# Attention steps of the engines shifted, and the scaling of the probabilities on GpSimd

## The chip, the core and the metric

One core of a Trainium2 chip runs the whole program. The metric is the device time of one execution in microseconds (us). Five engines run streams of their own and meet only in semaphores: TensorE (PE) multiplies and transposes, VectorE (DVE), ScalarE (ACT) and GpSimd (POOL) work on tiles of 128 partitions, SyncE (SP) issues most of the transfers. Inputs and results are f32 in HBM.

## The reference, cut to what matters

Two layers and one larger block over 512 positions of width 1024. Every attention that matters here is a softmax over at most 512 keys of each of 512 queries:

```python
s = einsum('bcqhd,bckhd->bhcqk', qc, kb) * (d ** -0.5)   # each layer: 6 heads "A" with a bias table,
s = where(valid, s + bias, NEG)                           # 5 heads "C" and 5 heads "B" (256 chosen keys)
p = jax.nn.softmax(s, axis=-1)
o = einsum('bhcqk,bckhd->bcqhd', p, vb)
# block 2: 16 heads "Fox", causal, with a decay
logits = einsum('bhqd,bhkd->bhqk', qi, k) * scale + (fi[..., :, None] - cum_f[..., None, :])
y_fox = softmax(where(k_pos <= q_pos, logits, -inf)) @ v
```

Around them stand feed-forward parts, projections of the input with `w_in`, a stick-breaking attention, a linear recurrence and gates; the change does not touch those.

## The kernel before, in words

**Numbers.** Each f32 product is made of three products of rounded parts (high times high, high times low, low times high; L214 to L216). So each operand is split: ScalarE writes the high part, another engine subtracts and writes the low part.

**Steps.** An attention is a list of steps, one for each head and each block of 128 queries. The four steps of a head have 128, 256, 384 and 512 keys (TT is 4). A layer runs 24 steps for heads A (`a_steps`) and, after the projection of C, 40 steps for heads C and B (`cb_steps`). Block 2 runs 64 steps for Fox (`fox_steps`). A step m goes through seven stages:

1. TensorE: the scores, three matmuls (L1012 to L1014), a fourth for Fox (L1016).
2. VectorE: mask, copy to SBUF, negated row maximum (L1094).
3. ScalarE: exponential with the row sum (L1057).
4. VectorE: reciprocal of the sum (L1101), drain (L1102), scaling of the probabilities in place (L1103).
5. TensorE: transposes of the blocks of 128 keys into a PSUM bank (L1039).
6. ScalarE: high part of the transposed block (L1074).
7. VectorE: low part (L1109).

After the four steps of a head TensorE makes the head's values from the transposed parts, twelve matmuls (L1028 to L1031).

**Order.** Each engine has its own function with a loop over n: `attend_pe_parts`, `attend_act_parts`, `attend_dve_parts`. In pass n of the kernel before, TensorE does the scores of step n, the values of a head when n is 3 mod 4, and the transposes of step n-3 (LAG is 3). ScalarE does the exponential of n, splits of the next pair of heads where n is 5 or 6 mod 8 (`split_act`), and the high part of n-3. VectorE does the row maximum of n, the scaling of n-1 and the low part of n-3. The transposes have two banks to turn in (`n_turned`), the probabilities four buffers (the row maximum of n waits for the transposes of n-4), and the transposed parts of a head one buffer for each part: the first high part of the next head waits for `hv_done`, the values of the head before. GpSimd makes the low parts of the split pairs (`split_pool`, L987), in the layers also the transfers of the bias table (`bias_dma`).

**What is woven in.** In heads A, VectorE also runs a round of the choice of B's keys in each of the first steps (`select_rounds`, maximum and replacement of eight, with drains) and the bias of each head (`bias_dve`). In Fox the attention is woven with 24 projections, "tiles" below, of 24 matmuls each: `woven` hands out a pass of the projection (`project_pe_parts` and its fellows), then a pass of the attention, on every engine in the same pattern; the projection's pass comes first. A projection's pass for tile j holds also what comes after for tiles j-1 and j-2: for a q or k tile a sum of squares on TensorE (L648), a root on ScalarE (L709) with a change of its function table before and after, reciprocal and spread on VectorE (L743, L746), transposes on TensorE (L630), and the scaling on VectorE (L733); for a v tile transposes (L660) and a copy (L756). VectorE's pass begins with the low part of a later weight tile (L206), which waits for ScalarE's high part (L199). Tiles come in the order q, k, v.

Of the kernel before, what the change touches and what calls it, by code (L numbers as in the profile page):

```python
# [16 lines left out]
F32 = mybir.dt.float32  # L17
# [69 lines left out]
def build(nc, A, out):  # L87
# [418 lines left out]
    pl_done = sem("probs_low_ready")  # L506
    hv_done = sem("head_values_used")
# [446 lines left out]
    class Places:  # L954

        def __init__(self, scores, turned, n_turned, probs, parts=None):
            self.scores, self.turned, self.n_turned, self.probs, self.parts = scores, turned, n_turned, probs, parts

# [10 lines left out]
    def layer_places(parts):  # L969
        return Places(lambda n, w: B[n % 2][:, 0:w], lambda m, a, b: B[2 + m % 2][:, a:b], 2,  # L970
                      lambda m, w: (SG[:, 0, 0:w], SG[:, 1, 0:w], TMP[:, 0:w], T[:, 0, 0:w])[m % 4], parts)
# [29 lines left out]

    def attend_pe_parts(pe, steps, n0, l0, h0, s0, y0, at, hook=None, banks=2):
        for n in range(len(steps) + LAG + 1):
# [14 lines left out]
            if n >= LAG + TT and (n - LAG) % TT == 0:  # L1018
                h = (n - LAG) // TT - 1
# [24 lines left out]
    def pair_taken(steps, n):  # L1044

        at = n - LAG - 8
        return at // 8 if at >= 0 and at % 8 == 0 else None

    def attend_act_parts(act, steps, n0, h0, s0, y_of, jobs, waits, at):
        act.drain()  # L1050
        pairs = len(jobs) // 3
        for n in range(len(steps) + LAG + 1):
            if n < len(steps):
# [4 lines left out]
                               accum_out=SUM[:, n % 4:n % 4 + 1]).then_inc(exp_done, 1)  # L1058
                pair = n // 8
# [8 lines left out]
            if LAG <= n < len(steps) + LAG:  # L1068
                m = n - LAG
                w = steps[m]["width"]  # L1070
                act.wait_ge(tr_done, n0 + (m + 3))
                if m % TT == 0:
                    act.wait_ge(hv_done, h0 + (m // TT + 1))
                act.activation(at.block(0, steps[m]), at.turned(m, 0, w).rearrange("p (k c) -> p k c", c=P), ACT.Copy  # L1074
                               ).then_inc(pt_done, 1)
            pair = pair_taken(steps, n)
            if pair is not None:
                act.wait_ge(hv_done, h0 + (2 * pair + 3))
                for bank, dst_hi, dst_lo in y_of(steps[8 * pair]["group"]):
                    act.activation(dst_hi, B[bank][:, :], ACT.Copy).then_inc(y_hi, 1)  # L1080
            yield

    def attend_dve_parts(dve, steps, n0, y0, y_of, at, hook=None):
        dve.drain()
        for n in range(len(steps) + LAG + 1):
# [19 lines left out]
            if LAG <= n < len(steps) + LAG:  # L1105
                m = n - LAG
                w = steps[m]["width"]
                dve.wait_ge(pt_done, n0 + (m + 3))
                dve.tensor_tensor(at.block(1, steps[m]), at.turned(m, 0, w).rearrange("p (k c) -> p k c", c=P),  # L1109
                                  at.block(0, steps[m]).bitcast(F32), ALU.subtract).then_inc(pl_done, 1)  # L1110
            pair = pair_taken(steps, n)
            if pair is not None:
# [256 lines left out]
    def layer_pool(pool, l):  # L1369
# [20 lines left out]
        for j in range(5, 9):  # L1390
            split_pool(pool, a_jobs, j, l * JOBS)
# [985 lines left out]
```

## Time and profile before

| what | value |
|---|---|
| median of 3 runs | 4385.77 us (4383.34 to 4387.92) |
| the profiled execution | 4383.03 us, its span 4381.4 us |
| TensorE busy | 4066.4 us, 93% of the span |
| VectorE busy | 1714.9 us, 39% |
| ScalarE busy | 1505.5 us, 34% |
| GpSimd busy | 369.0 us, 8% |
| mean granted TensorE clock | 0.926 |
| steps of heads A | 607 to 714 us and 1887 to 1996 us |
| steps of heads C and B | 751 to about 869 us and 2030 to 2151 us |
| steps of Fox | 2925 to 3247 us |

The span is cut into stages that follow each other. A share of busy time over the whole span says little of a stage, so each stage is read for itself: busy time and granted clock of its stretch first (the granted clock is 1.00 for 2.4 GHz and 0.50 for 1.2 GHz), then what its engines wait for, then the timeline of a few steps.

### The profile page before, as it was taken

How to read it: one execution, taken by the hardware profiler on the slowest of the kernel's cores; microseconds unless marked ns; L12 is line 12 of the kernel's file. 1: busy time of each engine (PE TensorE's matmuls, PEld its weight loads, DVE VectorE, ACT ScalarE, POOL GpSimd, SP SyncE). 2: the span in 40 equal slices, each digit the busy share in tenths (PEclk: the TensorE clock that was granted, in tenths of full speed). 3: DMA queues.
4: the chain of work that ended last, by engine and by line, in shares of the span. 5: the costliest groups of instructions: out<-in, count | busy, mean ns of one | idle time of the engine just before them, and what ended most of it. 6: DMA issues, size and time to landing. Idle time of an engine off the chain costs nothing.

```text
span 4381.4 us, 51384 instructions
## 1 busy us (share of the span) xinstructions
PE 4066.4 (93%) x17788; PEld 3216.0 (73%) x17788; DVE 1714.9 (39%) x2847; ACT 1505.5 (34%) x2448; POOL 369.0 (8%) x374
## 2 busy tenths in 40 slices
PE   8999978799999999967899989899999999789999
PEld 6887755588878887745688868787777668567888
DVE  3323565433323323664433234334432223534442
ACT  3222323432223223324332234435534553533331
POOL 1100011101001100011011000000100000100110
PEclk9999976799999999968799979999899999899999
DMA  3333310023323323200023324131112113222332
GB/s 102 96 97 97 82 42 20 1 82 96 96 82 91 96 96 93 76 19 20 29 82 96 96 86 112 39 83 44 39 54 72 39 44 91 58 73 76 96 98 98
DMA packets 495308, 316.51 MB, mean 72 GB/s; under 512 B 10832, under 2 KB 476368, under 8 KB 494640
## 3 DMA queue, kind: packets, MB, share of 16 engines
q1 hardware_dynamic: 490992, 302.86, 23.8%
q0 software_dynamic: 3008, 9.57, 0.7%
q8 instruction: 86, 1.41, 0.1%
q10 hardware_dynamic: 1152, 2.10, 0.1%
q14 instruction: 70, 0.57, 0.0%
HBM read 309.77 MB, written 4.33 MB: 72 GB/s over the span
## 4 chain that ended last, share of the span: by engine, by line
PE 68%; issue 21%; DVE 3%; ACT 3%; POOL 2%; PEld 1%; DVEq 1%; POOLq 0%; PEldq 0%; ACTq 0%
PE bank L214 19%; PE bank L216 19%; PE bank L215 19%; PE bank L256 1%; PE bank L1728 1%; PE bank L1734 1%; PE bank L1748 1%; PE bank L1737 1%; POOL h_lo L299 1%; PE bank L1028 1%; PE bank L1039 0%; PE bank L1030 0%; PE bank L1031 0%; PE bank L1149 0%; PE bank L648 0%
## 5 line engine op out<-in xcount | busy, mean ns | idle before, releaser
L214 PE MATMUL bank<-h_hi,w_hi 128*128 128x512 f32 (+3 forms) x3240 | 1297.9, 401 | 58.6 <-DVE w_lo L206 29.8
L215 PE MATMUL bank<-h_hi,w_lo 128*128 128x512 f32 (+3 forms) x3240 | 1279.0, 395 | 0.0
L216 PE MATMUL bank<-h_lo,w_hi 128*128 128x512 f32 (+3 forms) x3240 | 1277.7, 394 | 0.0
L206 DVE TENSOR_TENSOR w_lo<-w_raw,w_hi 128x1024 fp32r<-128x1024 f32 x571 | 737.7, 1292 | 1189.4 <-ACT w_hi L199 1183.4
L199 ACT ACTIVATE w_hi<-w_raw 128x1024 fp32r<-128x1024 f32 x571 | 598.4, 1049 | 596.4 <-DMA w_raw<-in_ffn_w_down 320.0
L214 PEld LDWEIGHTS bank<-h_hi,w_hi 128*128 128x128 f32 (+3 forms) x3240 | 612.1, 189 | 228.0 <-ACT lru_x L1831 31.0
L216 PEld LDWEIGHTS bank<-h_lo,w_hi 128*128 128x128 f32 (+3 forms) x3240 | 611.2, 189 | 140.5 <-issue 3.8
L215 PEld LDWEIGHTS bank<-h_hi,w_lo 128*128 128x128 f32 (+3 forms) x3240 | 612.5, 189 | 134.0 <-issue 4.6
L214 PE MATMUL bank<-g_hi,w_hi 128*128 (+1 forms) x880 | 342.3, 389 | 0.0
L215 PE MATMUL bank<-g_hi,w_lo 128*128 (+1 forms) x880 | 342.3, 389 | 0.0
L216 PE MATMUL bank<-g_lo,w_hi 128*128 (+1 forms) x880 | 342.3, 389 | 0.0
L383 POOL TENSOR_TENSOR g_lo<-gu_ring,g_hi 128x512 f32 x110 | 142.5, 1296 | 1048.2 <-ACT g_hi L357 838.5
L357 ACT ACTIVATE g_hi<-gu_ring 128x512 f32 x88 | 55.7, 632 | 424.0 <-DVE gu_ring L369 424.0
L215 PEld LDWEIGHTS bank<-g_hi,w_lo 128*128 128x128 f32 x880 | 165.2, 188 | 34.4
L214 PEld LDWEIGHTS bank<-g_hi,w_hi 128*128 128x128 f32 x880 | 165.2, 188 | 34.3
L216 PEld LDWEIGHTS bank<-g_lo,w_hi 128*128 128x128 f32 x880 | 165.2, 188 | 34.2
L256 PE MATMUL bank<-ones,s_ring 128*128 128x1 f32 x688 | 124.2, 316 | 38.5 <-ACT s_ring L241 33.2
L256 PEld LDWEIGHTS bank<-ones,s_ring 128*128 128x128 f32 x688 | 123.5, 283 | 43.4 <-ACT s_ring L241 34.6
L369 DVE TENSOR_TENSOR gu_ring<-s_ring,bank 128x512 f32<-128x512 f32 x88 | 60.5, 687 | 241.2 <-PE bank L216 241.2
L354 ACT ACTIVATE s_ring<-bank 128x512 f32<-128x512 f32 x88 | 52.7, 599 | 246.9 <-PE bank L216 246.9
L214 PE MATMUL bank<-branch_hi,w_hi 128*128 128x512 f32 x256 | 101.0, 394 | 13.4 <-POOL branch_lo L1930 13.4
L701 ACT ACTIVATE t_ring<-bank 128x512 f32<-128x512 f32 (+4 forms) x66 | 37.5, 569 | 199.1 <-PE bank L216 163.8
(382 smaller groups left out, 4404.1 us busy)
## 6 DMA issues: line engine op xcount, KB each, us to landing
w_raw<-in_w_in SPq DMA_DIRECT2D x161, 512.0 KB, 3.8
w_raw<-in_ffn_w_gate SPq DMA_DIRECT2D x88, 512.0 KB, 3.8
w_raw<-in_ffn_w_up SPq DMA_DIRECT2D x88, 512.0 KB, 3.8
w_raw<-in_ffn_w_down SPq DMA_DIRECT2D x88, 512.0 KB, 3.5
w_raw<-in_w_up SPq DMA_DIRECT2D x44, 512.0 KB, 3.7
w_raw<-in_w_branch SPq DMA_DIRECT2D x32, 512.0 KB, 3.8
w_raw<-in_w_out SPq DMA_DIRECT2D x24, 512.0 KB, 3.8
w_raw<-in_w_down SPq DMA_DIRECT2D x22, 512.0 KB, 3.5
```

The source lines that it names most:

```text
L199: act.activation(WH[:, slot(c), 0:w], RAW[:, slot(c), 0:w], ACT.Copy).then_inc(w_hi, 1)
L206: dve.tensor_tensor(WL[:, slot(c), 0:w], RAW[:, slot(c), 0:w], WH[:, slot(c), 0:w].bitcast(F32), ALU.subtract).then_inc(w_lo, 1)
L214: pe.matmul(bank, wh, xh, start=start, stop=False)
L215: pe.matmul(bank, wl, xh, start=False, stop=False)
L216: return pe.matmul(bank, wh, xl, start=False, stop=stop)
L256: last = pe.matmul(stat_bank[:, t:t + 1], SG[:, k % 2, t * P:(t + 1) * P], ONE[:, 0:1], start=(k == 0 and t == 0), stop=(k == n - 1), skip ...
L299: pool.tensor_tensor(dst[1](k), scaled_tile(k, n, width), dst[0](k).bitcast(F32), ALU.subtract).then_inc(nm_lo_odd, 1)
L354: act.activation(SG[:, t, :], B[2 * t][:, :], ACT.Silu).then_inc(silu_done, 1)
L357: act.activation(GH[:, i * 2 + t, :], GU[:, t, :], ACT.Copy).then_inc(gh_done, 1)
L369: dve.tensor_tensor(GU[:, t, :], SG[:, t, :], B[2 * t + 1][:, :], ALU.mult).then_inc(gu_done, 1)
L383: pool.tensor_tensor(GL[:, i * 2 + t, :], GU[:, t, :], GH[:, i * 2 + t, :].bitcast(F32), ALU.subtract).then_inc(gl_done, 1)
L1028: pe.matmul(out_, VH[:, kt, cols], at.keys(0, kt), start=(h % 2 == 0 and kt == 0), stop=False, skip_group_check=True)
```

## The change

A fifth function, `attend_pool`, runs on GpSimd, and the scaling of step n-1 moves to its pass n. It waits for the reciprocal (`rc_done`), and the drain ahead of the scaling goes. GpSimd's splits and the transfers of the bias table move into its passes. On the other engines the later stages move back. With n the pass:

| | before | after, layers | after, Fox |
|---|---|---|---|
| ScalarE, high part | n-3, after the splits | n-4, ahead of the splits; the first two steps of a head together in pass 1 mod 4 (`late`) | n-4, ahead of the splits |
| VectorE, low part | n-3, last in the pass | n-5, first in the pass; the first two steps together in pass 2 mod 4 | n-5, first in the pass |
| TensorE, values of a head | pass 3 mod 4 | pass 1 mod 4, two passes later | the same |
| TensorE, transposes of n-3 wait for the low part of | n-5 | n-6 (three banks) | n-5 (two banks) |

The tail has two passes more, and in Fox the 26 passes of the projection are spread over 70 instead of 68 passes.

```diff
     def layer_places(parts):
-        return Places(lambda n, w: B[n % 2][:, 0:w], lambda m, a, b: B[2 + m % 2][:, a:b], 2,
+        return Places(lambda n, w: B[n % 2][:, 0:w], lambda m, a, b: B[(2, 3, 6)[m % 3]][:, a:b], 3,
...
+    def turned_at(m, n, late):
+        if late and m % TT < 2:
+            return [] if m % TT == 0 else [k for k in (m - 1, m) if 0 <= k < n]
+        return [m] if 0 <= m < n else []
     def attend_pe_parts(pe, steps, n0, l0, h0, s0, y0, at, hook=None, banks=2):
-        for n in range(len(steps) + LAG + 1):
+        for n in range(len(steps) + TT + 2):
...
-            if n >= LAG + TT and (n - LAG) % TT == 0:
-                h = (n - LAG) // TT - 1
+            if n > 2 * TT and n % TT == 1:
+                h = n // TT - 2
...
-                pe.wait_ge(pl_done, l0 + (m + 1))
+                pe.wait_ge(pl_done, l0 + (m + 3 - at.n_turned))
...
     def attend_act_parts(act, steps, n0, h0, s0, y_of, jobs, waits, at):
...
+            for m in turned_at(n - TT, len(steps), at.late):
+                w = steps[m]["width"]
+                act.wait_ge(tr_done, n0 + (m + 3))
+                if m % TT == 0:
+                    act.wait_ge(hv_done, h0 + (m // TT + 1))
+                act.activation(at.block(0, steps[m]), at.turned(m, 0, w).rearrange("p (k c) -> p k c", c=P), ACT.Copy
+                               ).then_inc(pt_done, 1)
...
+    def attend_dve_parts(dve, steps, n0, y0, y_of, at, hook=None):
+        dve.drain()
+        for n in range(len(steps) + TT + 3):
+            for m in turned_at(n - TT - 1, len(steps), at.late):
...
                 dve.wait_ge(exp_done, n0 + (m + 1))
-                dve.reciprocal(RSUM[:, m % 4:m % 4 + 1], SUM[:, m % 4:m % 4 + 1])
-                dve.drain()
-                dve.tensor_scalar(at.probs(m, w), at.probs(m, w), RSUM[:, m % 4:m % 4 + 1], None,
-                                  ALU.mult).then_inc(nrm_done, 1)
+                dve.reciprocal(RSUM[:, m % 4:m % 4 + 1], SUM[:, m % 4:m % 4 + 1]).then_inc(rc_done, 1)
...
+    def attend_pool(pool, steps, n0, l0, s0, jobs, at, hook=None):
+        pairs = len(jobs) // 3
+        for n in range(len(steps) + 1):
+            if hook:
+                hook(pool, n)
+            if n >= 1:
+                m = n - 1
+                w = steps[m]["width"]
+                pool.wait_ge(rc_done, l0 + (m + 1))
+                pass_wait(pool)
+                pool.tensor_scalar(at.probs(m, w), at.probs(m, w), RSUM[:, m % 4:m % 4 + 1], None,
+                                   ALU.mult).then_inc(nrm_done, 1)
+            if n < len(steps):
+                pair = n // 8
+                if n % 8 == 5 and pair > 0:
+                    split_pool(pool, jobs, 3 * pair + 2, s0)
+                if n % 8 == 5 and pair + 1 < pairs:
+                    split_pool(pool, jobs, 3 * (pair + 1), s0)
+                if n % 8 == 6 and pair + 1 < pairs:
+                    split_pool(pool, jobs, 3 * (pair + 1) + 1, s0)
...
-    MEM_STEPS_AND_TAIL, FOX_STEPS_AND_TAIL = 16 + LAG + 3, 64 + LAG + 1
+    MEM_STEPS_AND_TAIL, FOX_STEPS_AND_TAIL = 16 + LAG + 3, 64 + TT + 2
```

## Rows read from the trace of the kernel before

**Rows 1.** Stretches of heads A, C and B, Fox: busy us (instructions) by engine, PE clock.
```profile
607.00:705.00 98.00, 70.62 (x190) 45.38 (x191) 60.53 (x173) 28.10 (x77) 12.54 (x14) 0.50 0.05 11
...
751.00:856.00 105.00, 75.03 (x306) 58.96 (x306) 56.41 (x193) 47.12 (x131) 20.60 (x16) 0.71 0.02 5
...
2925.00:3247.00 322.00, 305.31 (x1370) 238.20 (x1369) 146.93 (x397) 156.19 (x318) 26.76 (x21) 0.89 0.15 42
```

**Rows 2.** Waits of 751 to 856: engine, waited for, us in total, times, longest.
```profile
DVE cb_turned_lo L1109 <- ACT cb_turned_hi L1074: 42.3, 35, 3.4
...
PE bank L1028 <- DVE cb_turned_lo L1109: 22.8, 7, 5.6
```

**Rows 3.** Timeline in heads B: start us, us, engine, line, what, idle before.
```profile
819.97 0.55 DVE L1094 CUSTOM_DVE_ANT_0 tmp<-bank,b_select 128x384 f32<-128x384 f32 x1
...
820.55 0.61 ACT L1057 ACTIVATE tmp<-tmp,minus_row_max 128x384 f32<-128x384 f32 x1 [1.10 <-DVE minus_row_max L1094]
...
821.17 0.58 ACT L1074 ACTIVATE cb_turned_hi<-bank 128x512 fp32r<-128x512 f32 x1
821.78 0.69 DVE L1109 TENSOR_TENSOR cb_turned_lo<-bank,cb_turned_hi 128x512 fp32r<-128x512 f32 x1 [0.75 <-ACT cb_turned_hi L1074]
...
822.52 0.80 PE L1028 MATMUL bank<-cb_turned_hi,pair_v_hi 128*128 128x512 f32 x1 [2.60 <-DVE cb_turned_lo L1109]
...
825.80 0.29 PE L1039 MATMUL bank<-constants,s_ring 128*128 128x128 f32 x1
...
826.21 0.28 ACT L1074 ACTIVATE cb_turned_hi<-bank 128x128 fp32r<-128x128 f32 x1 [2.28 <-PE bank L1039]
```

**Rows 4.** VectorE's timeline, row maximum of step 4 and of step 36.
```profile
757.39 0.29 DVE L1094 CUSTOM_DVE_ANT_0 s_ring<-bank,mask 128x128 f32<-128x128 f32 x1
...
851.23 0.28 DVE L1094 CUSTOM_DVE_ANT_0 s_ring<-bank,mask 128x128 f32<-128x128 f32 x1
```

**Rows 5.** VectorE's timeline in heads A: a round, row maxima of steps 12 and 16.
```profile
661.60 0.68 DVE L861 MAX8 eight_largest<-b_select 128x8 f32<-128x512 f32 x1
...
663.79 0.29 DVE L1094 CUSTOM_DVE_ANT_0 s_ring<-bank,a_bias 128x128 f32<-128x128 f32 x1 [0.68 <-issue]
...
681.50 0.29 DVE L1094 CUSTOM_DVE_ANT_0 s_ring<-bank,a_bias 128x128 f32<-128x128 f32 x1 [0.32 <-issue]
```

**Rows 6.** Timeline in Fox after the matmuls of a k tile.
```profile
3059.91 0.95 PE L648 MATMUL bank<-half_indicators,s_ring 128*128 128x2 f32 x8
...
3062.80 1.28 ACT L1057 ACT_TABLE_LOAD   x1
...
3063.09 0.43 DVE L746 COPY tmp<-its_reciprocal 128x512 f32<-128x512 f32 x1
...
3066.20 0.78 PE L214 MATMUL bank<-h_hi,w_hi 128*128 128x512 f32 x1
```

**Rows 7.** Timeline in Fox after the v tile, then after the q tile.
```profile
3074.18 0.60 PE L630 MATMUL bank<-constants,tmp 128*128 128x128 f32 x4
...
3076.80 0.50 PE L1028 MATMUL bank<-fox_turned_hi,pair_v_hi 128*128 128x512 f32 x1
...
3078.14 0.43 DVE L746 COPY tmp<-its_reciprocal 128x512 f32<-128x512 f32 x1
...
3079.92 0.48 PE L214 MATMUL bank<-h_hi,w_hi 128*128 128x512 f32 x1
...
3085.48 0.60 PE L630 MATMUL bank<-constants,tmp 128*128 128x128 f32 x4
...
3086.78 0.68 DVE L756 COPY pair_v<-bank 128x512 f32<-128x512 f32 x1
```

**Rows 8.** Groups of GpSimd: count, busy us, mean ns, idle before.
```profile
L987 POOL TENSOR_TENSOR c_q_lo_parts<-c_q,two_q_hi 96x1024 fp32r<-96x1024 f32 x4 | 9.5, 2376 | 82.8 <-ACT two_q_hi L980 82.8
...
L1397 POOL COPY c_k<-c_k 32x512 f32<-32x512 f32 x8 | 4.5, 607 | 6.5 <-DVE minus_row_max L1094 6.5
...
L987 POOL TENSOR_TENSOR b_k_lo<-b_k,two_k_hi 128x512 fp32r<-128x512 f32 x4 | 5.1, 1267 | 2.6 <-ACT two_k_hi L980 2.6
```

More of the change, by code:

```diff
@@ L954, in build, with __init__ @@
     class Places:
-        def __init__(self, scores, turned, n_turned, probs, parts=None):
+        def __init__(self, scores, turned, n_turned, probs, parts=None, late=False):
             self.scores, self.turned, self.n_turned, self.probs, self.parts = scores, turned, n_turned, probs, parts
+            self.late = late
         def block(self, part, x):
@@ L969, in layer_places @@
     def layer_places(parts):
[L970 to L971 removed]
+        return Places(lambda n, w: B[n % 2][:, 0:w], lambda m, a, b: B[(2, 3, 6)[m % 3]][:, a:b], 3,
+                      lambda m, w: (SG[:, 0, 0:w], SG[:, 1, 0:w], TMP[:, 0:w], T[:, 0, 0:w])[m % 4], parts, late=True)
     IN_A, IN_CB = layer_places(PT_A), layer_places(PT_CB)
@@ L1051, in attend_act_parts @@
         pairs = len(jobs) // 3
-        for n in range(len(steps) + LAG + 1):
+        for n in range(len(steps) + TT + 2):
             if n < len(steps):
@@ L1058, in attend_act_parts @@
                                accum_out=SUM[:, n % 4:n % 4 + 1]).then_inc(exp_done, 1)
+            for m in turned_at(n - TT, len(steps), at.late):
[5 more added lines that the diff above has]
+                               ).then_inc(pt_done, 1)
+            if n >= 13 and n % 8 == 5:
+                pair = (n - 13) // 8
+                act.wait_ge(hv_done, h0 + (2 * pair + 3))
+                for bank, dst_hi, dst_lo in y_of(steps[8 * pair]["group"]):
+                    act.activation(dst_hi, B[bank][:, :], ACT.Copy).then_inc(y_hi, 1)
+            if n < len(steps):
                 pair = n // 8
@@ L1067, in attend_act_parts @@
                     split_act(act, jobs, 3 * (pair + 1) + 1, s0, waits(3 * (pair + 1) + 1))
[L1068 to L1080, printed above, removed]
             yield
@@ L1084, in attend_dve_parts @@
         dve.drain()
-        for n in range(len(steps) + LAG + 1):
+        for n in range(len(steps) + TT + 3):
+            for m in turned_at(n - TT - 1, len(steps), at.late):
+                w = steps[m]["width"]
+                dve.wait_ge(pt_done, n0 + (m + 3))
+                dve.tensor_tensor(at.block(1, steps[m]), at.turned(m, 0, w).rearrange("p (k c) -> p k c", c=P),
+                                  at.block(0, steps[m]).bitcast(F32), ALU.subtract).then_inc(pl_done, 1)
             if n < len(steps):
@@ L1100, in attend_dve_parts @@
                 dve.wait_ge(exp_done, n0 + (m + 1))
-                dve.reciprocal(RSUM[:, m % 4:m % 4 + 1], SUM[:, m % 4:m % 4 + 1])
-                dve.drain()
-                dve.tensor_scalar(at.probs(m, w), at.probs(m, w), RSUM[:, m % 4:m % 4 + 1], None,
-                                  ALU.mult).then_inc(nrm_done, 1)
[L1105 to L1112, printed above, removed]
+                dve.reciprocal(RSUM[:, m % 4:m % 4 + 1], SUM[:, m % 4:m % 4 + 1]).then_inc(rc_done, 1)
+            if n >= 14 and n % 8 == 6:
+                pair = (n - 14) // 8
                 for bank, dst_hi, dst_lo in y_of(steps[8 * pair]["group"]):
@@ L1398, in layer_pool @@
         pool.drain()
-        for j in range(len(cb_jobs)):
+        for j in range(3):
             split_pool(pool, cb_jobs, j, l * JOBS + len(a_jobs))
+        attend_pool(pool, cb_steps, l * N_STEPS + N_A, l * N_STEPS + N_A, l * JOBS + len(a_jobs), cb_jobs, IN_CB)
         norm_pool(pool, KT, l * N_T + 21, h_parts())
@@ L2179, in block2_pool @@
                 pool.dma_start((FQ, FK)[a // 2][a:P:32, c, :], dram_f[a, 4 * c:4 * c + 4, :]).then_inc(fq_in, 16)
-        for j in range(3, len(fox_jobs)):
-            split_pool(pool, fox_jobs, j, JF)
+        attend_pool(pool, fox_steps, SF, SPT, JF, fox_jobs, FOX_AT)
         sb_pool(pool)
```

17 lines of the change are left out of this document (8 added, 9 removed).

## The prediction

> **What bounds the kernel now.** I read the busy shares by stretch first. The whole span shows TensorE at 93%, but the three kinds of stretch that the change touches differ: TensorE is busy 70.6 of 98 us in heads A, 75.0 of 105 in heads C and B, 305 of 322 in Fox [rows 1]. So the first two kinds are set by something else, and Fox nearly by TensorE, with 17 us idle and a clock of 0.89. A chance of a gain lies in the layers, twice each; the danger lies in Fox.
>
> Next the waits. In C and B the low part on VectorE waits 42.3 us for ScalarE's high part, and TensorE's values wait 22.8 us for the low part [rows 2]. The timeline shows why: one step goes row maximum 819.97, exponential 820.55, high part 821.17, low part 821.78, and VectorE reaches the next row maximum some 0.6 us later [rows 3]. VectorE's scaling lies inside that loop under ScalarE's 1.2 us, so it costs nothing there. Once a head the loop also runs through TensorE: the values begin at 822.52 only when the last low part is there, after 2.6 us idle, the transposes of the next head stand behind them at 825.80, and ScalarE's high part at 826.21 [rows 3]. Eight heads take 851.23 - 757.39 = 93.8 us, 11.7 each [rows 4].
>
> **Part 1: the scaling on GpSimd.** GpSimd has no such instruction in the trace. Its subtraction of 128x512 takes 1.27 us, its copy of 32x512 0.6 [rows 8]. So a head of 1280 columns costs at least 1.5 us and at most 3.2, under a head's time everywhere. I take 1 us for 512 columns, between the two. VectorE loses the scaling and the drain, but they stood under ScalarE, so the gain is nil. What counts is the queue: the splits' low parts now stand between scalings. In pass 5 mod 8 GpSimd waits for ScalarE's splits, which now come after the high parts, does V and Q, scales step 5, does K in pass 6. In the pairs whose K has 1024 columns (2.38 us each, [rows 8]) K is ready near 10.9 us after the odd head's first low part, while TensorE would want it, for the scores of the next pair, near 6. Then the values of pass 9 come about 2.4 us late; with 512 columns 0.6 late. Two pairs of each kind: 6 us for each run of C and B. The bias transfers are issued passes ahead and hidden.
>
> The Trainium skill speaks against this part: GPSIMD Engine Reference, Performance versus the Vector engine, puts ordinary two-input work on GpSimd at about half VectorE's speed, and its engine selection table has one input roughly at line rate. The trace bears out the first with that 1.27 us, and shows no one-input multiplication. At 1.27 the scalings ahead of K take 0.2 us longer and the sum hardly moves. SBUF — State Buffer, Who interferes with whom, adds that a VectorE instruction with two SBUF inputs, as the weights' low part is, and a GpSimd one that reads SBUF shut each other out. Each of the five waits behind a k tile in part 4 could so grow by the length of one scaling, 5 us in all, which would make the sum 4417.
>
> **Part 2: the later stages, in C and B.** The loop maximum, exponential, high, low, maximum stays: the low part of n-5 stands ahead of the maximum of n and needs a high part that follows the exponential of n-1. What goes is one link of four, since the first two steps of a head are taken together, and TensorE's part of the loop. With the durations of the loop in rows 3, scaled by width, a head's four links are 0.55, 1.9, 2.2 and 2.65 us, 7.3 in all. Values begin 0.75 us after the last low part's start and last 3.3 us at the low clock [rows 3], near 2 at the full one (3076.80 to about 3078.8, [rows 7]). The high parts of the next head wait for them: 7.8 us a head at the full clock, 9.6 at the low one, where TensorE's own work also comes to 10.9. The clock was 0.71 [rows 1]; with TensorE denser I take most heads at the full one, 8.5. Splits and the copy of the pair's values hold ScalarE 1.2 us in each odd head, so 9.1. Gain (11.7 - 9.1) x 8 = 21 us, the last head and the tail of two more passes 2, less the 6 of GpSimd's queue: **17 us a run, 34 in both layers**, from 24 (low clock throughout) to 52.
>
> **Part 3: heads A.** There VectorE runs a round of the choice in each of the first 16 steps, 2.2 us with its drains [rows 5]. It lies in the loop before as after. Steps 12 to 16 take 17.7 us [rows 5]; by the same links, plus 2.2 for each round and 0.95 for the bias, I get 17.5 with a full set of rounds. Some 1 us a head is won, mostly since splits no longer stand between exponential and high part: 4. In the two heads without rounds the later values win 3.8 in one, and the second gives 0.5 and the tail 1 back. **6 us a run, 12 in all**, from 0 to 24.
>
> **Part 4: Fox.** Two differences from the layers decide. The transposes have two banks, so those of n-3 need the low part of n-5, which VectorE now makes in pass n and not n-2. And the projection's pass stands ahead of the attention's on each engine. After a k tile's matmuls end (3059.91), VectorE is busy with its root until 3063.09 + 0.43, so 3.6 us [rows 6]. After a v tile the spread ends at 3078.14 + 0.43, 4.4 us after 3074.18; after a q tile the copy is through 2.0 us after 3085.48 [rows 7]. Before, the low part needed by the transposes right after the tile was long made. Now the transposes wait for it. Walking eight steps with their three tiles, with the links of part 2:
>
> - after a v tile (pass 0 mod 8): scores done 2.0 us after its end, low part at 5.0: TensorE waits 3.1.
> - after a q tile: 0.5, then 0.3 and 1.8, for TensorE meets the low part of each further pass 2.4 us after the last one but has some 1.5 us of own work.
> - after a k tile, the worst: its 26 passes over 70 put it ahead of pass 5 mod 8 in every pair. ScalarE's pass 4 mod 8 ends in the high part of a new head, which waits for values that TensorE makes in pass 5, behind the tile. So ScalarE and, behind it, VectorE stand through the whole tile. Then come ScalarE's weight split, its two copies, the root with its table, VectorE's reciprocal, and only then the low part: 8.8 us after the tile's end against 3.7 for the end of the values. TensorE waits 5.2.
> - small ones, 1.3, and 0.9 from splits.
>
> That is 13 us idle for eight steps. There are five such groups, two with stick-breaking tiles (no root; waits of some 7 and 4) and the ends (5): 81 us, against 17 idle before, so +64. Before, the same walk gives 37 us for eight steps where [rows 1] give 322 / 8 = 40: the low clock after pauses costs 3 to 4. With three longer pauses I add 11 in all. **Fox +75 us**, from 48 (all at the full clock) to 98.
>
> A pause of TensorE of 2 to 5 us is what precedes 1.2 GHz in this profile: in C and B, values that begin after 2.6 us idle run 3.3 us [rows 3], in Fox those without a pause 2.0 [rows 7].
>
> **The sum.** 4383.0 (the profiled execution) + 75 - 34 - 12 = **4412 us**. The median of the runs shown is 2.7 us above that execution, well under the terms; I leave it in the range.
>
> **Rivals.**
>
> 1. *The layers win more than Fox loses.* Mechanism: in Fox the waits fall on time that TensorE spent at 1.2 GHz anyway, so that they overlap; in C and B the dense TensorE stays at the full clock. For it: the mean clock of 0.89 hides 35 us. Against: the wait behind the k tile is serial, ScalarE has work of its own after it. It decides once Fox loses less than the layers gain. Price: Fox +30, layers -60: **4353**. Chance 0.18.
> 2. *They cancel.* Fox +48, layers -46: **4385**. Chance 0.14.
> 3. *GpSimd becomes the bound.* If its scaling took 2.4 us for 512 columns, the time of its 1024-column subtraction [rows 8], a pair would cost it 12 + 6.3 us against 18 for the other engines: the gain of C and B goes, and Fox is as above: 4383 + 75 - 0 - 5 = **4453**. For it: no row shows the instruction. Against: one input less than the subtraction. Chance 0.10.
>
> My forecast has 0.58.
>
> **Range and chances.** The forecast's own bounds: all at the low ends 4383 + 48 - 76 = 4355, all high 4383 + 98 - 24 = 4457; not all fall together, and half of the terms' deviations gives 4384 to 4440. Taking in most of rivals 1 and 3: **4362 to 4452**. A measurement of this kernel can tell about 0.2%, 9 us, from no change. Faster by more than that: rival 1 and a little of the forecast's low end, 0.20. Within: 0.15. Slower: 0.65.
>
> **What would show it.** In C and B: 128-wide row maxima 8.5 to 9.5 us apart (11.7 now), and no idle of 2.6 us ahead of L1028. The busy time of a 512-column scaling on GpSimd near 1 us, and its K low part late in the 1024-column pairs. In A: distances of 17 to 18 us in the first four heads. In Fox: the stretch near 397 us, the transposes (L1039) idle for the low part of Fox some 60 us in all, with single waits of 5 us after k tiles, and ScalarE's high part of a 128-wide step waiting for L1031. Wrong would be: a Fox stretch under 365 us (then the order behind the tiles is not what I read), or scalings over 2 us, or waits of TensorE for `probs_ready` in the layers.

## The result, and the profile after

| | before | after |
|---|---|---|
| median, us | 4386.85 (4383.34 to 4391.35) | 4457.17 (4455.27 to 4467.08) |
| ratio, 95% interval | 1 | 1.0164 (1.0146 to 1.0183) |
| profiled execution, us (span) | 4383.03 (4381.4) | 4467.08 (4465.5) |

The changed kernel is slower by 70 us. The forecast had 4412 in a range of 4362 to 4452: the sign is right, the size is not, and the range ends 5 us too low. One execution below, of 11909 us in the run `shift_alone`, is left out as slow. The profiled execution of after is 10 us above its median. The terms below are differences of the two profiled executions, 84.1 us in all.

Where do they lie? I took the first row maximum of each stretch, and what follows the last one, as milestones:

| stage, us | before | after | difference | forecast |
|---|---|---|---|---|
| A, first row maximum to the projections of C, two layers | 99.4, 100.0 | 87.3, 87.4 | -12.1, -12.6 | -6, -6 |
| C and B, first row maximum to the output projection | 119.1, 118.6 | 113.9, 116.4 | -5.2, -2.1 | -17, -17 |
| Fox, first row maximum to the start of stick-breaking | 406.1 | 514.8 | +108.7 | +75 |
| all ahead of Fox's first row maximum | 2927.96 | 2903.24 | -24.7 | -46 |

The four layer terms sum to -32.0; 7.3 us were lost again in code that is the same in both, of which 4.9 lie ahead of the first heads A.

The stretches of after that answer to [rows 1], with 75.7 us idle in Fox. The Fox stretch runs from the first row maximum to about the end of the last values, which comes some 10 us behind the last row maximum before and some 16 after, where the tail has two passes more. Cut so, Fox is 318 us in the kernel before (2928 to 3246), 302.3 busy and 15.7 idle. Columns: length, busy us (instructions) of PE, PEld, DVE, ACT and POOL, then TensorE's granted clock.

```profile
614.00:706.00 92.00, 69.49 (x214) 45.58 (x213) 53.70 (x155) 28.17 (x80) 38.03 (x38) 0.59 0.05 12
747.00:844.00 97.00, 72.12 (x297) 56.45 (x295) 38.53 (x149) 45.61 (x128) 58.08 (x51) 0.71 0.00 1
2903.00:3328.00 425.00, 349.27 (x1349) 264.96 (x1349) 118.43 (x331) 154.91 (x316) 95.44 (x85) 0.76 0.11 31
```

So Fox's +107 between these cuts is **60.0 us of idle time and 47.0 us of busy time**, for the same matmuls. (With 10 us behind the last row maximum in both, it is 58 and 44.) The clock fell from 0.89 to 0.76.

TensorE's waits in Fox (us in total, times, longest) have one name:

```profile
PE bank L1047 <- DVE fox_turned_lo L1092: 73.7, 39, 5.0
PE bank L1036 <- DVE fox_turned_lo L1092: 1.8, 1, 1.8
```

The timeline behind a k tile, which answers to [rows 6]: start, duration, engine, line, what, and in brackets the idle time before it.

```profile
3084.61 0.95 PE L649 MATMUL bank<-half_indicators,s_ring 128*128 128x2 f32 x8
...
3088.20 0.27 PE L1039 MATMUL bank<-fox_turned_lo,pair_v_hi 128*128 128x128 f32 x1
3088.57 0.28 ACT L1067 ACTIVATE fox_turned_hi<-bank 128x128 fp32r<-128x128 f32 x1 [10.38 <-PE bank L1039]
3088.74 1.05 ACT L199 ACTIVATE w_hi<-w_raw 128x1024 fp32r<-128x1024 f32 x1
3089.69 0.59 ACT L699 ACTIVATE pair_k<-bank 128x512 f32<-128x512 f32 x1
3089.82 1.22 DVE L206 TENSOR_TENSOR w_lo<-w_raw,w_hi 128x1024 fp32r<-128x1024 f32 x1 [12.08 <-ACT w_hi L199]
3090.16 0.60 ACT L700 ACTIVATE s_ring<-bank 128x512 f32<-128x512 f32 x1
3090.78 1.28 ACT L710 ACT_TABLE_LOAD   x1
...
3092.66 0.43 DVE L747 COPY tmp<-its_reciprocal 128x512 f32<-128x512 f32 x1
3093.00 0.28 DVE L1092 TENSOR_TENSOR fox_turned_lo<-bank,fox_turned_hi 128x128 fp32r<-128x128 f32 x1
...
3093.43 0.87 PE L1047 MATMUL bank<-constants,fox_probs 128*128 128x128 f32 x3 [4.96 <-DVE fox_turned_lo L1092]
```

ScalarE has stood 10.4 us for the values, VectorE 12.1 for ScalarE. Both stood through the whole tile, and their work for it comes one after the other ahead of the low part. This is the chain of the prediction, and its 5.2 us.

Then the clock around a pause, in stretches of 1 us (same columns):

```profile
3109.00:3110.00 1.00, 0.45 (x3) 0.24 (x2) 0.00 (x0) 0.98 (x2) 0.00 (x0) 1.00 0.92 259
3110.00:3111.00 1.00, 0.00 (x0) 0.00 (x0) 0.00 (x0) 0.98 (x2) 0.00 (x0) 1.00 0.79 236
3111.00:3112.00 1.00, 0.00 (x0) 0.00 (x0) 0.90 (x3) 0.99 (x1) 0.00 (x0) 0.56 0.00 0
3112.00:3113.00 1.00, 0.52 (x2) 0.29 (x2) 0.61 (x4) 0.72 (x3) 0.18 (x1) 0.50 0.00 0
3113.00:3114.00 1.00, 1.00 (x4) 0.71 (x3) 0.00 (x0) 0.06 (x1) 1.00 (x1) 0.50 0.00 0
...
3116.00:3117.00 1.00, 1.00 (x5) 1.00 (x4) 0.00 (x0) 0.00 (x0) 0.00 (x0) 0.50 0.00 0
3118.00:3119.00 1.00, 0.19 (x2) 0.05 (x1) 0.41 (x2) 0.28 (x1) 0.00 (x0) 1.00 0.00 0
```

TensorE stops in 3109 and starts in 3112 again; the clock is at 1.2 GHz from 3111 on and back at 2.4 only in 3118, after 5 us of dense work. Summed over such stretches of 1 us, TensorE is busy at a clock under 0.75 for 63 of its 302 us in Fox before, and for 171 of 349 after. Work at half the clock takes about twice as long (in the projection tile of 3078 to 3084 products of 128x512 start 0.42 us apart at first and 0.22 later), so half of the difference, 54 us, is an estimate of what the low clock adds; 47 were measured.

In C and B the waits of 747 to 856 (us in total, times, longest) answer to [rows 2]:

```profile
PE bank L1020 <- POOL b_k_lo L989: 11.8, 3, 6.6
PE bank L1036 <- DVE cb_turned_lo L1092: 9.2, 6, 2.0
PE bank L1020 <- POOL c_k_lo_parts L989: 3.8, 1, 3.8
```

The values' wait fell from 22.8 to 9.2 us, as the change's shift makes one expect. In its place the scores wait 15.6 us for the next pair's K low part, 3.8, 6.6, 3.6 and 1.5 at the four pairs. The timeline of the second layer shows the queue ahead of it: on GpSimd V, Q, a scaling, K.

```profile
2087.87 1.29 POOL L989 TENSOR_TENSOR pair_v_lo<-b_v,pair_v_hi 128x512 fp32r<-128x512 f32 x1 [2.89 <-ACT pair_v_hi L982]
...
2089.10 1.29 POOL L989 TENSOR_TENSOR b_q_lo<-b_q,two_q_hi 128x512 fp32r<-128x512 f32 x1
...
2090.35 0.94 POOL L1127 TENSOR_SCALAR s_ring<-s_ring,row_sum_reciprocal 128x256 f32<-128x256 f32 x1
...
2091.24 1.28 POOL L989 TENSOR_TENSOR b_k_lo<-b_k,two_k_hi 128x512 fp32r<-128x512 f32 x1
...
2092.65 0.47 PE L1020 MATMUL bank<-two_k_hi,two_q_hi 64*128 64x128 f32 x1 [3.19 <-POOL b_k_lo L989]
```

The new instruction itself, as groups of GpSimd (count, busy us, mean ns):

```profile
L1127 POOL TENSOR_SCALAR t_ring<-t_ring,row_sum_reciprocal 128x512 f32<-128x512 f32 x32 | 50.0, 1563 | 35.0 <-DVE row_sum_reciprocal L1109 35.0
...
L1127 POOL TENSOR_SCALAR s_ring<-s_ring,row_sum_reciprocal 128x128 f32<-128x128 f32 x32 | 19.3, 602 | 18.1 <-DVE row_sum_reciprocal L1109 17.6
```

Its 1.56 us for 512 columns is above the two-input subtraction of the same size, 1.27 [rows 8], which the prediction took for a bound. VectorE had needed 0.49 us for it:

```profile
L1103 DVE TENSOR_SCALAR t_ring<-t_ring,row_sum_reciprocal 128x512 f32<-128x512 f32 x32 | 15.6, 487 | 2.5
```

In A, VectorE's timeline over one head answers to [rows 5]. It shows steps 8 to 12, for which the kernel before took 18.4 us; steps 12 to 16, those of [rows 5], went from 17.7 to 14.7:

```profile
644.92 0.29 DVE L1102 CUSTOM_DVE_ANT_0 s_ring<-bank,a_bias 128x128 f32<-128x128 f32 x1 [0.33 <-issue]
...
645.21 0.67 DVE L862 MAX8 eight_largest<-b_select 128x8 f32<-128x512 f32 x1
...
647.04 0.42 DVE L1102 CUSTOM_DVE_ANT_0 s_ring<-bank,a_bias 128x256 f32<-128x256 f32 x1 [0.33 <-issue]
...
648.30 0.70 DVE L1092 TENSOR_TENSOR a_turned_lo<-bank,a_turned_hi 128x128 fp32r<-128x128 f32 x2 [0.75 <-ACT a_turned_hi L1067]
...
660.33 0.29 DVE L1102 CUSTOM_DVE_ANT_0 s_ring<-bank,a_bias 128x128 f32<-128x128 f32 x1 [0.33 <-issue]
```

The head takes 660.33 - 644.92 = 15.4 us, where 17.5 were forecast for one with a full set of rounds. In the pass with no low part the round begins at once, at 645.21, beside ScalarE's exponential, and the next maximum comes 2.1 us after the last. In that pass the round is the loop and not an addition to it.

### The profile page after: what moved, and what is told of

It reads as the page before. It is cut to its first block, busy times and chain, and to the rows that moved or that the text cites. A ratio compares the mean times of both kernels' runs of the same rounds, so it can differ in the third digit from the quotient of the medians.

```text
span 4465.5 us, 51512 instructions
## 1 busy us (share of the span) xinstructions
PE 4125.5 (92%) x17788; PEld 3254.4 (73%) x17788; DVE 1635.5 (37%) x2655; ACT 1503.1 (34%) x2448; POOL 574.5 (13%) x566
## 4 chain that ended last, share of the span: by engine, by line
PE 74%; issue 14%; DVE 5%; ACT 3%; POOL 2%; DVEq 1%; PEld 1%; PEldq 0%; POOLq 0%; ACTq 0%
PE bank L214 20%; PE bank L215 20%; PE bank L216 20%; PE bank L256 1%; PE bank L1047 1%; PE bank L1749 1%; PE bank L1036 1%; PE bank L1755 1%; PE bank L1020 1%; PE bank L1039 1%; PE bank L1038 1%; PE bank L1769 1%; PE bank L1758 1%; POOL h_lo L299 1%; PE bank L1022 1%
```

## The experiments

Two theories stood at the start. **Mine**: in Fox the low part of the same pass, behind the work for a projection tile, holds the transposes, and each pause of TensorE brings a low clock; in C and B the late K eats the gain. **The rival**: GpSimd's scaling, half again dearer than I took it, is what everything waits for. The distances named below run from the first to the last row maximum of a stretch, as read from VectorE's timeline: before has A 87.8, C and B 105.4 and 104.8, Fox 307.8; after has 75.1, 100.3 and 103.4, 410.1. Each ratio is taken against runs of the kernel before on the same chip (medians 4383 to 4386 us).

**One part in one place.** Three kernels take the change apart.

```diff
 # layers as changed, Fox as before
     FOX_AT = Places(..., 2, ..., PT_X,
+                    shift=False, gp=False)
 # the shift alone: the scaling stays on VectorE, all passes shifted
+                if not at.gp:
+                    dve.drain()
+                    dve.tensor_scalar(at.probs(m, w), at.probs(m, w), RSUM[:, m % 4:m % 4 + 1], None,
+                                      ALU.mult).then_inc(nrm_done, 1)
 # GpSimd alone: attend_pool as changed, all other steps in the passes of before, two banks in the layers
```

> The layers run as in the changed kernel, Fox as in the kernel before (values in pass 3 mod 4, three-pass lag, scaling on VectorE). By the two traces Fox lost 109 us (first row maximum to the start of stick-breaking: 406 to 515 us) and everything ahead of it won 25. Theory (the two parts do not act on each other): 4387 - 25 = about 4360 us, from 4350 to 4370, and the Fox stretch is again some 109 us shorter than in the changed kernel. Rival (part of Fox's loss is carried in from the layers, by the clock or by late weights): the time stays above 4380.

Measured: 4346.5 us, ratio 0.9911 (0.9897 to 0.9925). Fox takes 307.4 us again, A 75.1. The layers' gain stands alone, and it is 39 us by the medians, 32 by the two profiled executions: more than the 25 I had read, since those had lost some 7 in common code. Against the changed kernel this is 110.7 us less, which is Fox's whole loss. The two parts don't act on each other, as expected; the time came out 3.5 us under the range of 4350 to 4370.

> Only the shifted passes, in the layers and in Fox; the scaling stays on VectorE, behind the reciprocal and a drain, in the same pass as before. GpSimd has the splits alone. Theory A (Fox loses by the low part standing behind VectorE's and ScalarE's work for a projection tile): Fox loses 90 to 115 us as in the changed kernel, the waits of the transposes for the low part stay near 74 us. In C and B the next pair's K low part is no longer late on GpSimd (15 us of waits of the scores in one run of the changed kernel), so the layers win some 15 us more: about 4435 us. Theory B (GpSimd's scaling, 1.56 us for 512 columns, is what Fox and the layers wait for): Fox is within 20 us of before, and the whole near 4345 us.

Measured: 4456.9 us (three executions), 1.0165 (1.0144 to 1.0186), the time of the changed kernel within 1 us. In its Fox stretch, then TensorE's wait for the low part there:

```profile
2894.00:3316.00 422.00, 346.25 (x1350) 262.59 (x1349) 147.17 (x395) 154.94 (x316) 26.48 (x21) 0.77 0.12 31
```

```profile
PE bank L1051 <- DVE fox_turned_lo L1102: 73.6, 39, 5.0
```

The same 39 waits, the same longest one, to 0.1 us in the sum, with no scaling on GpSimd at all. That ends the rival for Fox. C and B take 97.3 and 97.7 us, 3 and 6 less than with the scaling on GpSimd; the K is still waited for, but 11.8 us instead of 15.6. A takes 78.4, 3 more. The total missed my 4435: I expected 15 us from C and B and got 9, and the two runs of A gave back 7.

> Only the scaling on GpSimd, in the layers and in Fox; every other step in the pass where the kernel before has it, two banks for the transposes. Theory A: in Fox it costs little, -5 to +15 us, since the scaled weights are needed two passes later; in C and B the K low part is late behind scalings, +5 to +15 us a run: 4390 to 4420 us in all. Theory B (GpSimd is the cause in Fox): Fox alone loses 60 us or more, the whole over 4450 us.

Measured: 4386.1 us, 1.0003 (0.9992 to 1.0015), no difference. Fox 303.7 us (-4), A 84.8 and 84.6 (-3), C and B 107.4 and 104.9 (+2 and 0). Moving the scaling is small everywhere, with its sign set by what VectorE and GpSimd otherwise do there. What moved the time was the shift: -9 in each A, -8 in each C and B, +99 in Fox.

**What a pause costs.** The kernel before, with TensorE held in Fox by a multiplication on a tile that nobody reads; all waits of the changed kernel are absent.

```diff
+            if n < len(steps) and n > 0 and n % 4 == 0:        # TensorE, behind the transposes
+                pe.wait_ge(held, held_count(n))
+            pool.wait_ge(tr_done, SF + (n - LAG + 3))          # GpSimd
+            for i in range(5 if n % 8 == 4 else 3):
+                pool.drain()
+                last = pool.tensor_scalar(HELD[:, :], MASK[:, 0:256], ONE[:, 0:1], None, ALU.mult)
+            last.then_inc(held, 1)
```

> The kernel before with TensorE held 15 times in Fox, after the transposes of passes 4 mod 8 and 0 mod 8, until GpSimd has done five or three multiplications of 256 columns (0.93 us each by the changed kernel's trace, with a drain each) on a tile that nobody reads: some 5 and 3 us, about 60 us in all. Nothing else of Fox's order changes. Theory A (a pause costs itself and then a low clock): the Fox stretch grows by 90 to 110 us, TensorE's busy time in it by 35 to 50 us, its mean granted clock falls from 0.89 to near 0.78. Theory B (the clock in Fox of the changed kernel fell for another reason than the pauses): the stretch grows by 60 us or less and the busy time stays near 305 us.

Measured: 4480.7 us, 1.0223 (1.0203 to 1.0243); Fox 403.6 us, +95.8. The waits and the stretch:

```profile
PE bank L1022 <- POOL held_work L1068: 44.8, 9, 6.0
PE bank L214 <- POOL held_work L1068: 32.0, 6, 8.2
```

```profile
2930.00:3344.00 414.00, 325.42 (x1365) 250.73 (x1366) 149.18 (x396) 156.67 (x318) 88.75 (x82) 0.82 0.12 32
```

The pauses were longer than planned, 76.8 us in 15. Idle time grew by 72.9 us (88.6 against 15.7), busy time by 23.1. The stretch is within theory A's 90 to 110 us, the busy time in neither theory's range: it did grow, so a pause costs more than itself, but by less than the 35 us that I set as the least. Work at the low clock is 109 us (63 before); half of the difference is 23, which again is the whole growth. Per pause it is 1.5 us. The changed kernel has 39 waits for the low part, so the next run took the number of pauses apart from their length.

> The kernel before with TensorE held 45 times in Fox, after the transposes of three passes in four, each time for one multiplication of 256 columns on GpSimd with a drain: by the run with 61 such multiplications in 15 pauses (76.8 us of waits, 1.26 each) some 1.3 us a pause, 57 us in all. Theory A (what lowers the clock is the number of pauses): TensorE's busy time in Fox grows by 40 us or more, the stretch by 95 to 110 us. Theory B (a pause of 1.3 us leaves the clock high, only those of 2 us and more lower it): busy time grows by 0 to 15 us, the stretch by 50 to 70 us.

```diff
-            if n < len(steps) and n > 0 and n % 4 == 0:
+            if 4 <= n < 64 and n % 4 != 3:                     # one multiplication each
```

Measured: 4479.6 us, 1.0211 (1.0191 to 1.0231); Fox 398.3 us, +90.5.

```profile
PE bank L1022 <- POOL held_work L1070: 35.5, 28, 1.5
PE bank L214 <- POOL held_work L1070: 28.3, 17, 3.4
```

```profile
2930.00:3338.50 408.50, 342.64 (x1351) 259.50 (x1352) 151.07 (x395) 155.15 (x316) 69.98 (x66) 0.79 0.12 33
```

Less idle time than with the long pauses (50 us more than before, not 73), but 40.3 us more busy time, not 23. The stretch is 5 us under what theory A gave, its busy time is at the threshold of A and far from B's. Pauses of 1.3 us bring a low clock too, and 45 short ones cost more clock than 15 long ones. The prediction had read pauses of 2 to 5 us ahead of the low clock. Side by side: the changed kernel's Fox has +60 idle and +47 busy from 39 waits, this one +50 and +40 from 45. So the kernel before, given such pauses and nothing else of the change, shows a clock term of the size of the changed kernel's.

**Is it the order behind a tile, or the two banks?** Three variants of the changed kernel's Fox.

```diff
 # attention ahead of the tile, on every engine
+            next(a, None)
             if (i + 1) * n_b // n_a > i * n_b // n_a:
                 next(b, None)
-            next(a, None)
 # three banks, the third taken from the projection
-    FOX_AT = Places(..., lambda m, a, b: B[2 + 2 * (m % 2)][:, a:b], 2,
+    FOX_AT = Places(..., lambda m, a, b: B[(2, 4, 7)[m % 3]][:, a:b], 3,
...
-    banks=WOVEN
+    banks=WOVEN_SB     # Banks((5,), (6,)): one bank for the later stages
```

> The changed kernel, and in Fox each engine takes the attention's pass ahead of the projection's pass instead of behind it (the order of the two in the weave). Theory (the low part stands behind the tile's square root, reciprocal and spread, that is why the transposes wait): the waits of the transposes for the low part fall from 74 us to under 35, the clock recovers with them, and the whole is near 4385 us, from 4360 to 4410. Rival (the low part two passes later with two banks is too late in any order): waits over 60 us, the whole over 4435 us.

Measured: 4468.4 us, 1.0184 (1.0164 to 1.0203).

```profile
PE bank L1054 <- DVE fox_turned_lo L1105: 85.2, 42, 6.6
```

No gain: waits and time are those of the rival (over 60 us, over 4435). The rival was stated too broadly, though, and so was the experiment: a weave is a ring. Where all engines exchange the two, a tile still stands between pass n-1 and pass n everywhere, and only another pass is its neighbour. So this run says little about the cause. The next one changes the order for two engines only:

> The changed kernel, and in Fox ScalarE and VectorE take the attention's pass ahead of the projection's, while TensorE keeps the projection's ahead. (Exchanged on all engines, the tile still stood between the same kind of passes, and the waits were 88 us instead of 74.) So the low part that the transposes behind a tile need no longer stands behind the tile's copies, square root and spread. Theory (that work is what the transposes wait for): waits for the low part under 35 us, low clock less, near 4390 us, from 4360 to 4415. Rival (the attention's own loop, maximum, exponential, high and low part, is what is late with two banks): waits over 60 us, over 4440 us.

Measured: 4515.6 us, 1.0296 (1.0279 to 1.0313), the slowest of all.

```profile
PE bank L1054 <- DVE fox_turned_lo L1105: 126.2, 33, 6.6
```

The theory behind it falls: taking the tile's work from ahead of the low part doesn't free the transposes. That work now begins only after the exponential of a pass whose scores stand behind the tile, and the low part of the next pass stands behind it in turn, as long as 6.6 us. Wherever ScalarE's and VectorE's work for a tile is put, with two banks each pass's transposes need a low part of the same pass, and the work lies between two of those. What remains is to need an older one:

> The changed kernel, and in Fox the transposes rotate over three PSUM banks; the third is taken from the projection's later stages, which keep one of their two. The transposes of a pass then need the low part that VectorE made in its previous pass, not in this one. Theory (two banks are what turns the shift into a wait): waits for the low part under 20 us, low clock as in the kernel before, near 4375 us, from 4350 to 4400. Rival (the values, four passes behind, or the projection with one bank make a wait of their own of the same size): over 4420 us.

Measured: 4401.5 us, 1.0033 (1.0020 to 1.0045), 55.6 us less than the changed kernel; Fox 354.3 us.

```profile
PE bank L1051 <- DVE fox_turned_lo L1102: 21.7, 9, 3.5
PE bank L649 <- DVE pair_q L734: 5.6, 6, 0.9
PE bank L661 <- issue: 5.3, 6, 0.9
```

One more bank takes 52 of the 73.7 us of waits, at the price of 11 us of new ones where the projection has one bank for its later stages. That is a little above what I expected (4350 to 4400): waits of 22 us, not under 20, and Fox is still 47 us above before. So two banks under a low part made two passes later are shown to be the cause of at least 56 of Fox's 102 us. Of the rest, the stretch 2901 to 3270 shows 35.6 us idle (20 more than before) and 333.4 busy (31 more); which of the nine remaining waits come from the values four passes behind wasn't taken apart.

**C and B: the late K, and the clock.** Both start from the kernel with shifted layers and Fox as before.

```diff
 # K ahead of V, ScalarE and GpSimd alike; the counts that TensorE waits for follow
-    pass 5 mod 8: V of this pair, Q of the next      pass 6: K of the next
+    pass 5 mod 8: Q of the next                      pass 6: K of the next, V of this pair
```

> As the kernel with shifted layers and Fox as before (4346 us), and in the layers ScalarE and GpSimd split the next pair's Q in pass 5 mod 8, then its K, then this pair's V in pass 6, in place of V, Q, K. In C and B of that kernel the scores wait 17 us a run for the K low part. Theory (the late K is what holds the next pair up): 6 to 12 us a run are won, 4322 to 4334 us, and the distance of 128-wide row maxima over an odd head falls by some 2.5 us. Rival (the loop of row maximum, exponential, high and low part ends last anyway, K is only late beside it): under 2 us a run, 4342 to 4350 us, with the waits moved to the low part of the weights.

Measured: 4346.6 us, 0.9901 (0.9885 to 0.9917), no change of the median. Yet C and B take 96.9 and 97.1 us, 6 less a run, at a granted clock of 0.74, with the wait for K down from 17.0 to 12.9 us:

```profile
741.00:845.00 104.00, 79.97 (x306) 62.38 (x305) 40.75 (x156) 47.07 (x132) 60.16 (x54) 0.66 0.02 5
```

```profile
743.00:840.00 97.00, 73.67 (x302) 58.26 (x303) 40.35 (x156) 47.10 (x132) 58.82 (x53) 0.74 0.01 3
```

The first row is of the kernel it starts from. The stretch won what the theory said, with 4 us less waiting for K and 6 us less TensorE time. By the profiled executions 6.3 us of it went again between the last row maximum of the first C and B and the first of the second layer's A, in code that is the same: 1034.3 us there against 1040.6. Over the profiled executions of all fourteen kernels this part takes from 1034.3 to 1041.1 us, and the kernel it starts from has the lowest, so this difference needs no cause in the new order. The stretch bears the theory out; that the whole kernel gains is not shown.

```diff
 # one more product a pass in C and B, into a bank that nobody reads there
+                pe.matmul(B[7][:, :], HH[:, 0, 0:P], HH[:, 0, :], start=True, stop=True)
```

> As the kernel with shifted layers and Fox as before (4346 us), and in each pass of C and B TensorE makes one more product of 128x512 behind the scores, into a bank that nobody reads there: 0.4 us at full clock, 0.8 at the low one, 40 a run. Without them TensorE is busy 80 of 104 us at a granted clock of 0.66. Theory A (the clock is low because TensorE pauses, and filled pauses keep it up): the granted clock in C and B rises over 0.85, and the run of C and B, first to last row maximum, is 94 to 102 us against 103. Theory B (the gaps are not filled where it counts): the clock stays under 0.75 and the filling is paid for: 110 to 125 us a run.

Measured: 4352.4 us, 0.9926 (0.9911 to 0.9942); C and B 101.3 and 101.8 us.

```profile
740.00:841.00 101.00, 78.77 (x344) 60.66 (x342) 39.82 (x155) 46.98 (x132) 59.57 (x53) 0.81 0.01 2
```

Some 40 products more, and TensorE is busy 1.2 us less than without them. The clock rose from 0.66 to 0.81, short of 0.85, and the stretch is within A's bounds. So the clock is low there because TensorE pauses, and it costs TensorE about as much as 40 products. But the run of C and B gained only 2 us by it (103.4 and 103.2 before the filling): a higher clock, paid for with 40 products, hardly helps it. That its loop runs through the other engines was not tested by itself.

**The parts where they pay.** Shifted passes in the layers only, the scaling on GpSimd in A and Fox and on VectorE in C and B; then K ahead of V as well.

> Shifted passes in A, C and B, none in Fox; the scaling on GpSimd in A and in Fox, on VectorE in C and B. From single parts measured so far, first to last row maximum: C and B 97.5 us with the scaling on VectorE against 103 on GpSimd, Fox 303.7 against 307.4 on VectorE, A 75.1 against 78.4. Theory (the stretches add up): 4346 - 2 x 5.7 - 4 = about 4331 us, from 4325 to 4338. Rival (the order on GpSimd doesn't matter in C and B, the differences between those runs are of the clock's phase): within 4 us of 4346.

Measured: 4340.6 us, 0.9891 (0.9874 to 0.9907). C and B 97.8 and 96.3, Fox 303.8, A 74.8 and 74.6: each stretch has its number, but the median shows 6 of the 15 us. It lies just above theory's range.

> As the kernel with shifted layers, scaling on GpSimd in A and in Fox, on VectorE in C and B, and Fox unshifted (4341 us), and in the layers K split ahead of V. Theory (with the scaling on VectorE the late K of C and B, some 12 us of waits a run, comes from ScalarE's order, and the new order takes a part of it): 2 to 5 us a run, 4330 to 4337 us. Rival (without scalings on GpSimd the K is bound by ScalarE's pass, the order changes nothing): 4337 to 4345 us.

Measured: 4333.1 us, 0.9897 (0.9881 to 0.9913); C and B 93.7 and 93.5 us.

```profile
740.00:834.00 94.00, 69.80 (x304) 55.79 (x302) 61.19 (x194) 47.57 (x132) 18.96 (x16) 0.78 0.02 4
```

The theory's range holds the median, and the stretch won 4 and 3 us. In the whole this gain is not shown: the five executions go from 4332.1 to 4349.4 us, and the ratio, 0.9897, is no lower than the 0.9891 of the kernel without K ahead. It is the lowest median of all kernels here, 50 us under before and 124 under the change as made; by the ratios this kernel and the one above can't be told apart.

## Why the prediction was wrong in size

**What bounds the kernel**: right. The danger lay in Fox, the gain in the layers, and each part did there what its sign said.

**Part 4, Fox, idle time**: right, step by step. Idle was forecast to grow by 64 us and grew by 60. The single waits were 5.0 us behind a k tile (5.2), 3.0 and 0.8 behind a v tile (3.1 and the small ones), 0.3, 0.35 and 1.75 behind a q tile (0.5, 0.3 and 1.8), and ScalarE's high part of a 128-wide step stood through the tile as described.

**Part 4, the clock**: here the sum broke. "With three longer pauses I add 11 in all" should have been 47. I had the mechanism, a pause of TensorE comes before 1.2 GHz, and priced it by the 3 to 4 us per eight steps of the kernel before, as if three long pauses were few. The runs show what should have been counted, the short pauses too: 15 pauses of 5 us cost 23 us of additional busy time, 45 of 1.4 us cost 40. The upper bound for Fox, 98, was passed too, by 109 measured. With 47 in place of 11 the Fox term is 111, and the sum 4448; with the 24.7 us won ahead of Fox in place of 46 it is 4469, against 4467 of the profiled execution.

**Part 1, the scaling on GpSimd**: the price, 1 us for 512 columns, was wrong, and so was the bound from the subtraction: 1.56 measured. That alone cost little: the run with GpSimd alone is level with before. For one input the Trainium skill, GPSIMD Engine Reference, engine selection, says roughly line rate; this case's rows disagree, with 1.56 us on GpSimd against 0.49 on VectorE. The waits, which the prediction would have let grow by the length of a scaling, were 73.6 us without and 73.7 with the scaling on GpSimd. VectorE's low part of a weight tile does get longer beside GpSimd's two-input subtraction: in the kernel before 110 of the 571 took 1.6 us, each begun while such a subtraction ran, where most take 1.23.

```profile
1000.29 1.30 POOL L383 TENSOR_TENSOR g_lo<-gu_ring,g_hi 128x512 f32 x1 [9.48 <-ACT g_hi L357]
1001.07 1.59 DVE L206 TENSOR_TENSOR w_lo<-w_raw,w_hi 128x1024 fp32r<-128x1024 f32 x1 [1.75 <-ACT w_hi L199]
...
1005.67 1.23 DVE L206 TENSOR_TENSOR w_lo<-w_raw,w_hi 128x1024 fp32r<-128x1024 f32 x1 [3.00 <-ACT w_hi L199]
```

So the rule cited, of the Trainium skill, SBUF — State Buffer, Who interferes with whom, is borne out by this trace for two-input work. For the scaling, which reads SBUF too, the changed kernel has one such meeting, the weight tile at 2915.22, and that took 1.23 us: no effect there.

**Part 1, the queue**: right mechanism, wrong size. I put 6 us a run on the late K, and the scores waited 15.6. I took the pairs of 1024 columns as 2.4 us late and those of 512 as 0.6; they were 3.8 and 6.6, and 3.6 and 1.5. The rows at 2087.87 to 2092.65 show a wait of 3.2 us for 512 columns, as ScalarE's splits begin only behind the values and the pair's copy. Even without scalings in the queue 11.8 us remained.

**Part 2, C and B**: forecast -17, measured -5.2 and -2.1. Besides the K, "with TensorE denser I take most heads at the full one" failed: the clock stayed at 0.71 and 0.65 (747 to 844 and 2010.6 to 2114.1). The waits for K are pauses too, and the filling products show that pauses keep it low there. The values' wait fell as said. The low end of the range, 12 a run, was not low enough.

**Part 3, A**: forecast -6, measured -12.1 and -12.6. I added a round's 2.2 us to each of four passes; in the pass without a low part it lies beside the exponential.

**The rivals**: rival 3 has a time near the result, 4453, mostly by another road: it lets all of the gain of C and B go, and 7 of 34 us were left, but the scaling took 1.56 us and not 2.4, GpSimd was busy in 58 of 97 us, and with the scaling back on VectorE only 9 us more were won there. Fox grew without it. Rival 1's first half, waits that fall on time spent at 1.2 GHz anyway, is the reverse of what happened: they made more of it.

**The signs named**: A's first heads came out at 10.2 and 14.7 to 15.6 us and not 17 to 18, C's and B's, but for the first of a run, at 10 to 13.7 and not 8.5 to 9.5, the scaling at 1.56 and not near 1. Of the three signs of being wrong, one is there in small: TensorE waits for the scaling in the layers, 1.5 us between 747 and 856. In Fox the single waits behind k tiles and ScalarE's wait for the values are as named; the transposes waited 73.7 us and not some 60, and the stretch is 425 us, where 318 + 75 = 393 were forecast on this cut.

**The range**: half of the deviations is 4384 to 4434, not 4440; the stated range doesn't hang on it.

## What to carry to other kernels

Where TensorE is nearly the bound, count the pauses that a new order gives it, and price each with the work at half clock that follows it, not with its length alone. When a stage is put later, look for the buffer that the early stages need back: two banks that were ample for a low part in pass n-2 made TensorE wait in 39 of Fox's passes, and one more bank took 52 of the 73.7 us of waits away. And try a change that touches several stretches in one stretch at a time: this one was worth 39 us in the layers and cost 111 in Fox.

## What the runs showed of the hardware

- GpSimd's multiplication by a per-partition scalar took 0.60, 0.92, 1.24 and 1.56 us for 128, 256, 384 and 512 columns, dearer at 512 than its two-input subtraction (1.27), and 3.2 times VectorE's 0.49.
- 45 pauses of some 1.4 us cost TensorE 40 us of additional busy time, 15 pauses of some 5 us 23. Half of the additional busy time at the low clock gave this growth within 7 us in each case (54 against 47 in the changed kernel, 23 against 23, 42 against 40).
- VectorE's low part of a 128x1024 weight tile took 1.6 us 110 times in the kernel before, each while GpSimd's two-input subtraction was under way, and 1.23 in most others.
- Forty additional products of 128x512 in C and B left TensorE's busy time where it was (80.0 and 78.8 us), as the granted clock rose from 0.66 to 0.81.
